# RWKV sample rows stored head by head and loaded with one transfer behind the first four cache pages

## The chip, the cores and the metric

The kernel runs on one core of a Trainium2 chip. A core has TensorE (PE: matrix products and transposes), VectorE (DVE), ScalarE (ACT) and GpSimd (POOL), and SyncE (SP), which here does nothing but wait on semaphores and issue DMA transfers; sixteen DMA engines move the data between the chip's main memory (DRAM or HBM) and the on-chip SBUF. The metric is the device time of one execution in microseconds (us). Two kernels are told apart by medians over several runs.

## The reference

One inference step of a two-layer hybrid trunk for a prompt of 256 tokens and for eight sample sequences of four tokens each. Each layer has three branches (SSD, RWKV-7, latent attention), gated and merged, and then a convolutional feed-forward network. Everything is float32. The part around the change is the RWKV recurrence of the sample sequences, and the paged attention of the same sequences that runs beside it:

```
D_MODEL, DEPTH, DEC_BATCH, DEC_SEQ = 1024, 2, 8, 4
RWKV_HEADS, RWKV_HEAD_DIM = 16, 64
PAST_LEN, PAGE_SIZE, MLA_KV_RANK, MLA_ROPE = 2048, 128, 256, 64     # 16 pages a sequence
def step(s, inp):                                  # rwkv_mixer, one token, state (b, h, v, k)
    r_t, w_t, k_t, v_t, kk_t, a_t = inp            # six vectors of 64 for each sequence and head
    sa = jnp.einsum('bhvk,bhk->bhv', s, -kk_t)
    s = (s * w_t[:, :, None, :] + sa[..., None] * (kk_t * a_t)[:, :, None, :]
         + v_t[..., None] * k_t[:, :, None, :])
    return s, jnp.einsum('bhvk,bhk->bhv', s, r_t)
s_fin, y = lax.scan(step, s0, (tm(rh), tm(wh), tm(kh), tm(vh), tm(kk), tm(ah)))
...                                                # then a normalization per head, bonus, gate
def page_step(carry, phys):                        # sample_mla: one page of 128 cached keys
    c, kr = lat_pool[phys], rope_pool[phys]
    k = mla_keys(c, kr, p['mla_w_kb'], p['mla_k_norm_g'])
    return update(carry, jnp.einsum('bqhe,blhe->bhql', q, k) * scale, c), None
carry, _ = lax.scan(page_step, init, page_table.T)
```

## The kernel before

`hybrid_trunk` loops over the two layers on the chip. A layer is a row of stages, each a block in which every engine has its own written list of instructions; engines wait for each other by named semaphores, and all of them meet at a barrier between two blocks. The order of work on an engine is therefore the order of the code. Four stages matter here, in this order.

`mla_prompt` is the attention of the prompt. Beside it TensorE transposes the sample tokens' six RWKV vectors, and VectorE copies them into `sample_rows` (32 rows, 6 vectors, 1024 columns). SyncE waits for the twelve copies (`row_kept`), stores the rows to the DRAM scratch `scratch_vec` (L707) and waits until they have landed; the block ends no earlier.

`mla_absorb` is short; SyncE loads the page table there.

`cache_attention` is the paged attention: eight sequences of 16 pages. Pages live in two slots, each a whole sequence, with four semaphores of four pages each. SyncE's `load(b, slot, g)` reads four page numbers and issues two transfers a page (L1052 latents, 128 KB; L1053 rotary keys, 32 KB). It loads both slots first, 32 pages, then the RWKV vectors into `vec` (L1060: 48 transfers, one for each sequence and vector, each of 16 heads by 4 tokens by 64), then `rwkv_state` (L1062, 2 MB), and then, as TensorE frees them, the pages of the other six sequences. For each page TensorE transposes (L1087, L1090), makes keys (L1112) and scores (L1116); ScalarE and VectorE square and sum the keys; the softmax of a sequence is done in pieces beside the pages of the next one (`finish`), and for the last sequence in a tail of its own, up to L1152. POOL waits for all 49 transfers (`rows_back`) and then runs the whole recurrence (`rwkv_sample_pool`, 304 instructions) on 128 partitions, one for each sequence and head, sequence-major. When it is done, SyncE stores the state (L1070).

`ssd_project` streams eleven weight blocks of 1 MB through a ring of three: SyncE loads, ScalarE rounds (L284), VectorE takes the rest (L290), TensorE multiplies (L297 to L299). Between them SyncE stores the normalized RWKV output `vec_y` to `scratch_y` in eight transfers (L1352), and loads it back as rows (L1356) for TensorE, which transposes it after the fifth block.

Of the kernel before, what the change touches and what calls it, by code (L numbers as in the profile page):

```python
# [28 lines left out]
P = 128  # L29
# [4 lines left out]
NB = 8  # L34
NS = 4
# [649 lines left out]
def mla_prompt(nc, k):  # L685
# [3 lines left out]
    with Stage(nc) as st:  # L689
# [13 lines left out]
        with st.block() as block:  # L703
            @block.sync
            def _(sp):
                sp.wait_ge(row_kept, 12)
                sp.dma_start(k.d["scratch_vec"].rearrange("t n d -> t n d"), rows[:, :, :]).then_inc(rows_out, 16)  # L707
                sp.wait_ge(rows_out, 16)

            @block.tensor  # L710
            def _(pe):
# [245 lines left out]
def cache_attention(nc, k):  # L957
# [19 lines left out]
    with Stage(nc) as st:  # L977
# [67 lines left out]
        with st.block() as block:  # L1045
            @block.sync
            def _(sp):
                def load(b, slot, g):
                    for j in range(4 * g, 4 * g + 4):
                        page = sp.value_load(k.pages[0:1, ds(b * PAGES + j, 1)], min_val=0, max_val=NPOOL - 1)  # L1050
                        row = ds(page, 1)
                        sp.dma_start(lat[:, slot, j, 0:KVRANK], k.ldram("cache_kv_latent")[row].rearrange("o p r -> (o p) r")).then_inc(in_l[slot][g], 16)  # L1052
                        sp.dma_start(kpe[:, slot, j, :], k.ldram("cache_k_rope")[row].rearrange("o p r -> (o p) r")).then_inc(in_l[slot][g], 16)  # L1053
                for slot in range(2):
                    for g in range(4):
                        load(slot, slot, g)

                for b in range(NB):
                    for n in range(6):
                        sp.dma_start(k.vec[16 * b:16 * b + 16, n, :, :],  # L1060
                                     k.d["scratch_vec"][NS * b:NS * b + NS, n, :].rearrange("t (h d) -> h t d", d=64)).then_inc(rows_back, 16)
                sp.dma_start(k.state[:, :, :], k.ldram("state_rwkv").rearrange("b h v k -> (b h) v k")).then_inc(rows_back, 16)  # L1062
                with sp.Fori(1, NB // 2) as i:
                    for slot in range(2):
                        for g in range(4):
                            sp.wait_ge(outed, i * (2 * GROUPS) + ((slot - 2) * GROUPS + g // 2 + 1))
                            load(i * 2 + slot, slot, g)

                sp.wait_ge(pool_step, POOL_STEPS)
                sp.dma_start(k.ldram("s_rwkv").rearrange("b h v k -> (b h) v k"), k.state[:, :, :]).then_inc(rwkv_out, 16)  # L1070
                sp.wait_ge(rwkv_out, 16)

            @block.gpsimd
            def _(pool):
                pool.wait_ge(rows_back, 16 * (6 * NB + 1))
                assert rwkv_sample_pool(nc, k, pool, pool_step) == POOL_STEPS

            @block.tensor
# [225 lines left out]
def ssd_project(nc, k):  # L1304
# [6 lines left out]
    with Stage(nc) as st:  # L1311
# [25 lines left out]
        with st.block() as block:  # L1337
            @block.sync
            def _(sp):
# [4 lines left out]
                for u in range(1, NU + 1):  # L1344
# [3 lines left out]
                                 w[:, ORDER[u] * G * P:(ORDER[u] + 1) * G * P].rearrange("(t p) n -> p t n", p=P)).then_inc(loaded[u % RING], 16)  # L1348
                    if u == RING - 1:
                        sp.wait_ge(normed, 1)  # L1350
                        for b in range(NB):
                            sp.dma_start(k.d["scratch_y"][NS * b:NS * b + NS, :].rearrange("t (h d) -> h t d", d=64),  # L1352
                                         k.vec_y[16 * b:16 * b + 16, :, :]).then_inc(y_out, 16)
                    if u == RING:
                        sp.wait_ge(y_out, 16 * NB)
                        sp.dma_start(sam_rows[:, :], k.d["scratch_y"]).then_inc(y_back, 16)  # L1356
                sp.wait_ge(rows_kept, 3)
                sp.dma_start(k.ldram("p_ssm_conv").rearrange("o j c -> (o j) c"), rows[0:3, :]).then_inc(stored, 16)
                sp.dma_start(k.ldram("s_ssm_conv").rearrange("b j c -> (b j) c"), rows[3:3 + 3 * NB, :]).then_inc(stored, 16)
# [1889 lines left out]

def hybrid_trunk(nc, dram):  # L3250
    k = Kit(nc, dram)
    with ExitStack() as ctx:
        def sb(name, shape, dt=F32):
            return ctx.enter_context(nc.sbuf_tensor(name, shape, dt))
# [57 lines left out]
```

## Time and profile before

| | |
|---|---|
| median of 3 runs | 3094.15 us (3092.66 to 3096.87) |
| span of the profiled execution | 3093.2 us |
| TensorE busy | 2765.1 us (89%) |
| VectorE, ScalarE, POOL busy | 1796.3, 1354.4, 840.5 us |
| cache attention, first layer | first page transfer at 460.53, last matmuls at 949.26 us |
| POOL's recurrence, first layer | 549.34 to 931.81 us |
| first transfer of the stage behind the prompt attention (`page_ids`) | 442.37 us |

The time of the profiled execution is its span, from the first to the last instruction, and what little lies around it; the span is 0.95 us under the median of the runs. Times in the rows are microseconds from the start of the span. PE is TensorE's matmuls, PEld its weight loads, a name with q behind it (SPq) the sequencer that issues DMAs. An instruction's row ends, in brackets, with the idle time before it and with whom it waited for.

### The profile page before, as it was taken

What the parts mean: (1) busy time and instruction counts of PE and PEld (TensorE: products, weight loads), DVE (VectorE), ACT (ScalarE), POOL (GpSimd) and SP (SyncE); (2) the same over time, 40 slices, a digit from 0 to 9 for tenths busy, and PEclk for the clock granted to TensorE, in tenths of its full rate; (3) what the DMA queues carried; (4) which work ended last, traced back from release to release, by engine and by line L of the source; (5) the groups of instructions that cost most, each with busy time, mean ns of one, the idle gap of its engine ahead of it and who ended that gap; (6) DMA issues with size and microseconds to landing.
All of it is one profiled execution on the core that took longest, in us unless ns stands there. A gap on an engine that the chain in (4) does not pass through costs nothing. (4 is left out here: it accounts for less than half of the span.)

```text
span 3093.2 us, 62907 instructions
## 1 busy us (share of the span) xinstructions
PE 2765.1 (89%) x24800; PEld 2537.1 (82%) x24800; DVE 1796.3 (58%) x3035; ACT 1354.4 (44%) x2174; POOL 840.5 (27%) x696
## 2 busy tenths in 40 slices
PE   7887779999997889899988867699999988898998
PEld 6876349999997779899977863499999886798998
DVE  4845454656655755499348453455565556554993
ACT  4733344445444343354356334344454443433542
POOL 0030000899990400000000300009999804000000
PEclk9999979999998989999989998799999989999999
DMA  5302102211115276465453021131211142764644
GB/s 132 101 5 81 46 15 75 63 50 54 35 35 177 71 197 166 106 163 139 119 123 84 4 80 46 26 92 39 57 43 39 54 157 78 204 164 109 163 134 119
DMA packets 471235, 281.94 MB, mean 91 GB/s; under 512 B 65294, under 2 KB 466489, under 8 KB 470315
## 3 DMA queue, kind: packets, MB, share of 16 engines
q1 hardware_dynamic: 468724, 276.85, 32.2%
q8 instruction: 190, 3.11, 0.4%
q10 hardware_dynamic: 2232, 1.26, 0.2%
q14 instruction: 89, 0.72, 0.1%
HBM read 258.75 MB, written 19.29 MB: 90 GB/s over the span
## 5 line engine op out<-in xcount | busy, mean ns | idle before, releaser
L1112 PE MATMUL key_banks<-w_kb_head,latent_T_head 128*128 128x352 f32 x1536 | 518.8, 338 | 0.0
L1112 PE MATMUL key_banks<-w_kb_rest,latent_T_head 128*128 128x352 f32 x1536 | 497.0, 324 | 0.0
L1112 PE MATMUL key_banks<-w_kb_head,latent_T_rest 128*128 128x352 f32 x1536 | 496.6, 323 | 0.0
L290 DVE TENSOR_TENSOR w_rests<-w_ring,w_heads 128x2048 fp32r<-128x2048 f32 (+1 forms) x152 | 326.3, 2149 | 163.9 <-ACT w_heads L284 163.7
L931 POOL TENSOR_TENSOR rwkv_state_tmp<-rwkv_state,vec 128x1024 f32<-128x1024 f32 x64 | 153.3, 2395 | 654.0 <-DMA rwkv_state<-in_state_rwkv_dram 649.1
L1257 DVE TENSOR_REDUCE w_kb<-key_sq 128x8 f32<-128x1024 f32 x256 | 309.3, 1208 | 0.0
L1172 ACT CAST latent_T_head<-turn_bank 128x256 fp32r<-128x256 f32 x256 | 95.5, 373 | 471.3 <-PE turn_bank L1090 298.5
L284 ACT CAST w_heads<-w_ring 128x2048 fp32r<-128x2048 f32 (+1 forms) x152 | 272.2, 1793 | 61.1 <-ACT conv_last_rows L1798 19.7
L1112 PEld LDWEIGHTS key_banks<-w_kb_rest,latent_T_head 128*128 128x128 f32 x1536 | 291.3, 190 | 0.0
L1112 PEld LDWEIGHTS key_banks<-w_kb_head,latent_T_head 128*128 128x128 f32 x1536 | 290.7, 189 | 0.0
L1112 PEld LDWEIGHTS key_banks<-w_kb_head,latent_T_rest 128*128 128x128 f32 x1536 | 290.0, 189 | 0.0
L2713 POOL TENSOR_TENSOR L_level<-L,const 128x1024 f32<-128x1024 f32 x24 | 56.3, 2367 | 855.8 <-DVE L L2719 802.5
L1188 ACT ACTIVATE key_sq<-key_banks 128x1056 f32<-128x1056 f32 x256 | 273.1, 1067 | 8.4 <-PE key_banks L1116 8.4
L1243 DVE TENSOR_TENSOR latent_T_rest<-turn_bank,latent_T_head 128x256 fp32r<-128x256 f32 x256 | 108.3, 423 | 269.4 <-ACT w_kb L1174 185.6
L297 PE MATMUL ffn_banks<-h_heads_T,w_heads 128*128 128x288 f32 x704 | 212.7, 302 | 17.1 <-DVE h_rests_T L1814 13.8
L298 PE MATMUL ffn_banks<-h_rests_T,w_heads 128*128 128x288 f32 x704 | 209.5, 298 | 0.0
L299 PE MATMUL ffn_banks<-h_heads_T,w_rests 128*128 128x288 f32 x704 | 208.6, 296 | 0.0
L934 POOL TENSOR_TENSOR rwkv_state_tmp<-rwkv_state_tmp 128x512 f32<-128x512 f32 (+4 forms) x320 | 196.7, 615 | 25.1
L297 PE MATMUL merge_banks<-out_heads,w_heads 128*128 128x288 f32 x512 | 152.1, 297 | 5.2 <-DVE out_rests L1620 5.2
L298 PE MATMUL merge_banks<-out_rests,w_heads 128*128 128x288 f32 x512 | 152.4, 298 | 0.0
L299 PE MATMUL merge_banks<-out_heads,w_rests 128*128 128x288 f32 x512 | 152.3, 297 | 0.0
L297 PEld LDWEIGHTS ffn_banks<-h_heads_T,w_heads 128*128 128x128 f32 x704 | 133.2, 189 | 21.5 <-DVE w_rests L290 17.8
(567 smaller groups left out, 7140.1 us busy)
## 6 DMA issues: line engine op xcount, KB each, us to landing
w_ring<-in_ffn_w_up_dram SPq DMA_DIRECT2D x88, 512.0 KB, 4.9
latents<-in_cache_kv_latent_dram SPq DMA_DIRECT2D x256, 128.0 KB, 2.0
w_ring<-in_w_in_dram SPq DMA_DIRECT2D x52, 512.0 KB, 3.7
w_ring<-in_w_gate_dram SPq DMA_DIRECT2D x48, 512.0 KB, 3.9
w_ring<-in_w_in_dram SPq DMA_DIRECT2D x20, 1024.0 KB, 6.0
w_ring<-in_ffn_w_down_dram SPq DMA_DIRECT2D x32, 384.0 KB, 3.6
w_ring<-in_ffn_w_down_dram SPq DMA_DIRECT2D x32, 320.0 KB, 4.1
rope_keys<-in_cache_k_rope_dram SPq DMA_DIRECT2D x256, 32.0 KB, 1.8
```

Of the source, the lines that this page charges most:

```text
L284: nc.scalar.copy(heads[:, slot, 0:tiles * P], ring[:, slot, 0:tiles * P]).then_inc(rounded, 1)
L290: ops.tensor_tensor(rests[:, slot, 0:tiles * P], ring[:, slot, 0:tiles * P], heads[:, slot, 0:tiles * P].bitcast(F32), ALU.subtract).then_ ...
L297: nc.tensor.matmul(out, wh, xh, start=start, stop=False)
L298: nc.tensor.matmul(out, wh, xl, start=False, stop=False)
L299: return nc.tensor.matmul(out, wl, xh, start=False, stop=stop)
L931: c(nc.gpsimd.tensor_tensor(tmp, S, over_v(n, t), ALU.mult))
L934: c(nc.gpsimd.tensor_tensor(tmp[:, :, 0:w], tmp[:, :, 0:w], tmp[:, :, w:2 * w], ALU.add))
L1112: last = nc.tensor.matmul(kbank[:, 3 * x + n, 0:KB], c[:, x, r * P:(r + 1) * P], w[:, r, cols], start=r == 0 and m == 0, stop=r == 1 and m ...
L1172: last = nc.scalar.copy(ch[:, x, :], xbank[:, 0:2 * P])
L1188: nc.scalar.activation(sq[:, x, :], kbank[:, 3 * x:3 * x + 3, 0:KB], ACT.Square).then_inc(squared, 1)
L1243: nc.vector.tensor_tensor(cl[:, x, :], xbank[:, 0:2 * P], ch[:, x, :].bitcast(F32), ALU.subtract).then_inc(t_kept, 1)
L1257: nc.vector.tensor_reduce(ss[:, slot, j, :], sq[:, x, f:f + KW].rearrange("p (h e) -> p h e", e=NOPE), AX.X, ALU.add).then_inc(summed, 1)
```

## The change

The scratch tensors get another layout and the partitions of `vec`, `rwkv_state` and `vec_y` another order. In `scratch_vec` a vector is now kept head by head (vector, head, row, 64 columns) and in `scratch_y` the output likewise (head, row, 64). SBUF partitions count head-major (head, then sequence), not sequence-major. With that, `vec` is loaded by one transfer with 1 KB pieces, in place of 48. The rows are stored by six transfers in place of one, in pieces of 64 values; the state is loaded and stored by eight transfers, one for each sequence; `vec_y` is stored by one in place of eight and loaded back in 64-value pieces. And the loads of `vec` and `rwkv_state` move forward: they stand behind the first four pages of slot 0, ahead of the other 28.

```
@@ mla_prompt, block.sync
                 sp.wait_ge(row_kept, 12)
-                sp.dma_start(k.d["scratch_vec"].rearrange("t n d -> t n d"), rows[:, :, :]).then_inc(rows_out, 16)
-                sp.wait_ge(rows_out, 16)
+                for n in range(6):
+                    sp.dma_start(k.vec_rows[n].rearrange("h r d -> r h d"),
+                                 rows[:, n, :].rearrange("r (h d) -> r h d", d=64)).then_inc(rows_out, 16)
+                sp.wait_ge(rows_out, 96)
@@ cache_attention, block.sync
+                load(0, 0, 0)
+                sp.dma_start(k.vec[:, :, :, :].rearrange("p n t d -> p n (t d)"),
+                             k.vec_rows.rearrange("n h (b t) d -> (h b) n (t d)", b=NB)).then_inc(rows_back, 16)
+                for b in range(NB):
+                    sp.dma_start(k.state[b:P:NB, :, :].rearrange("p v k -> p (v k)"),
+                                 k.ldram("state_rwkv")[b:b + 1].rearrange("b h v k -> (b h) (v k)")).then_inc(rows_back, 16)
                 for slot in range(2):
-                    for g in range(4):
+                    for g in range(1 - slot, 4):
                         load(slot, slot, g)
-
-                for b in range(NB):
-                    for n in range(6):
-                        sp.dma_start(k.vec[16 * b:16 * b + 16, n, :, :],
-                                     k.d["scratch_vec"][NS * b:NS * b + NS, n, :].rearrange("t (h d) -> h t d", d=64)).then_inc(rows_back, 16)
-                sp.dma_start(k.state[:, :, :], k.ldram("state_rwkv").rearrange("b h v k -> (b h) v k")).then_inc(rows_back, 16)
...
                 sp.wait_ge(pool_step, POOL_STEPS)
-                sp.dma_start(k.ldram("s_rwkv").rearrange("b h v k -> (b h) v k"), k.state[:, :, :]).then_inc(rwkv_out, 16)
-                sp.wait_ge(rwkv_out, 16)
+                for b in range(NB):
+                    sp.dma_start(k.ldram("s_rwkv")[b:b + 1].rearrange("b h v k -> (b h) (v k)"),
+                                 k.state[b:P:NB, :, :].rearrange("p v k -> p (v k)")).then_inc(rwkv_out, 16)
+                sp.wait_ge(rwkv_out, 16 * NB)
@@ cache_attention, block.gpsimd
-                pool.wait_ge(rows_back, 16 * (6 * NB + 1))
+                pool.wait_ge(rows_back, 16 * (1 + NB))
@@ ssd_project, block.sync
                         sp.wait_ge(normed, 1)
-                        for b in range(NB):
-                            sp.dma_start(k.d["scratch_y"][NS * b:NS * b + NS, :].rearrange("t (h d) -> h t d", d=64),
-                                         k.vec_y[16 * b:16 * b + 16, :, :]).then_inc(y_out, 16)
+                        sp.dma_start(k.y_by_head.rearrange("h (b t) d -> (h b) t d", b=NB), k.vec_y[:, :, :]).then_inc(y_out, 16)
                     if u == RING:
-                        sp.wait_ge(y_out, 16 * NB)
-                        sp.dma_start(sam_rows[:, :], k.d["scratch_y"]).then_inc(y_back, 16)
+                        sp.wait_ge(y_out, 16)
+                        sp.dma_start(sam_rows[:, :].rearrange("r (h d) -> r h d", d=64), k.y_by_head.rearrange("h r d -> r h d")).then_inc(y_back, 16)
@@ hybrid_trunk
+    k.vec_rows = dram["scratch_vec"].rearrange("r n c -> (r n c)").rearrange("(n h r d) -> n h r d", n=6, h=16, d=64)
+    k.y_by_head = dram["scratch_y"].rearrange("r c -> (r c)").rearrange("(h r d) -> h r d", h=16, d=64)
```

SyncE's order is all that moves; the other engines' lists keep theirs. At the start of the cache attention, before the change, SyncE goes from the last of the 32 pages (latents and rotary keys) to the 48 vector loads and the state, and then into the loop over the later sequences:

```order
L1052 DMA latents<-in_cache_kv_latent_dram 128x256
L1053 ISA
L1053 DMA rope_keys<-in_cache_k_rope_dram 128x64
L1060 DMA vec<-scratch_vec 16x4x64 x48
L1062 ISA
L1062 DMA rwkv_state<-in_state_rwkv_dram 128x4096
L1063 UNCONDITIONAL_BRANCH
```

After the change, these are the rows behind the fourth page; the transfer pair of `rwkv_state` stands eight times, of which two are shown here, and page 4 follows (TENSOR_LOAD reads its number):

```order
L1054 DMA latents<-in_cache_kv_latent_dram 128x256
L1055 ISA
L1055 DMA rope_keys<-in_cache_k_rope_dram 128x64
L1057 DMA vec<-scratch_vec 128x6x256
L1060 ISA
L1060 DMA rwkv_state<-in_state_rwkv_dram 16x4096
...
L1060 ISA
L1060 DMA rwkv_state<-in_state_rwkv_dram 16x4096
L1052 TENSOR_LOAD page_ids
```

What moved: 49 transfers behind 32 pages became nine transfers behind four pages, ahead of 28.

In the SSD projection, before the change, the eight stores stand between the third and the fourth weight block (`w_ring`):

```order
L1347 DMA w_ring<-in_w_in_dram 128x8x256
L1352 DMA scratch_y<-vec_y 16x4x64 x8
L1347 ISA
L1347 DMA w_ring<-in_w_in_dram 128x8x256
L1356 DMA sam_y_rows<-scratch_y 32x1024
```

After it, one store stands there:

```order
L1351 DMA w_ring<-in_w_in_dram 128x8x256
L1355 DMA scratch_y<-vec_y 128x256
L1351 ISA
L1351 DMA w_ring<-in_w_in_dram 128x8x256
L1358 DMA sam_y_rows<-scratch_y 32x16x64
```

The places are the same; seven transfers ahead of the fourth block are gone, and the load back has smaller pieces.

## Rows read from the trace of the kernel before

**Rows 1.** Waits, whole execution (us in total, times, longest).
```profile
POOL rwkv_state_tmp L931 <- DMA rwkv_state<-in_state_rwkv_dram: 649.1, 2, 325.3
```

**Rows 2.** SyncE timeline, cache attention (start us, us, instruction).
```profile
460.53 0.37 SPq L1052 DMA_DIRECT2D latents<-in_cache_kv_latent_dram  x1
...
466.37 0.33 SPq L1053 DMA_DIRECT2D rope_keys<-in_cache_k_rope_dram  x1
...
467.53 0.33 SPq L1052 DMA_DIRECT2D latents<-in_cache_kv_latent_dram  x1
...
517.23 23.91 SPq L1060 DMA_DIRECT2D vec<-scratch_vec  x48
```

**Rows 3.** POOL timeline, first and last of the layer.
```profile
549.34 2.38 POOL L931 TENSOR_TENSOR rwkv_state_tmp<-rwkv_state,vec 128x1024 f32<-128x1024 f32 x1 [323.78 <-DMA rwkv_state<-in_state_rwkv_dram]
...
931.59 0.22 POOL L936 TENSOR_TENSOR vec_y<-rwkv_state_tmp 128x16 f32<-128x16 f32 x1
```

**Rows 4.** TensorE timeline, page 4's transposes and the stage's last matmuls.
```profile
483.02 0.42 PE L1087 MATMUL turn_bank<-const,latents 128*128 128x128 f32 x2
...
949.26 5.78 PE L1152 MATMUL misc_bank<-qa,w_vb 128*128 128x32 f32 x32 [0.71 <-DVE qa L1294]
```

**Rows 5.** DMA issues (line, count, KB each, median us to landing).
```profile
rope_keys<-in_cache_k_rope_dram SPq DMA_DIRECT2D x256, 32.0 KB, 1.8
...
rwkv_state<-in_state_rwkv_dram SPq DMA_DIRECT2D x2, 2048.0 KB, 7.9
...
scratch_vec<-sample_rows SPq DMA_DIRECT2D x2, 768.0 KB, 5.3
...
out_dram<-kpe_tm SPq DMA_DIRECT2D x2, 64.0 KB, 1.7
...
out_dram<-kpe_tm SPq DMA_DIRECT2D x2, 8.0 KB, 1.4
```

**Rows 6.** Waits of TensorE, 457 to 956 us.
```profile
PE turn_bank L1087 <- DMA rope_keys<-in_cache_k_rope_dram: 12.2, 1, 12.2
...
PE misc_bank L1124 <- DVE w_kb L1280: 7.1, 1, 7.1
...
PE misc_bank L1127 <- ACT w_kb L1213: 3.9, 8, 0.7
```

**Rows 7.** VectorE, lines L1271, L1276, 470 to 956 us (ns min/median/max).
```profile
L1271 DVE TENSOR_TENSOR w_kb<-w_kb,rope_sumsq x8: 279/754/2482, 533.0 to 935.2; 128x128 f32<-128x128 f32 x8
...
L1276 DVE TENSOR_TENSOR w_kb<-w_kb x8: 681/1270/2535, 542.8 to 937.6; 128x512 f32<-128x512 f32 x8
```

**Rows 8.** Windows (stretch, busy us of each engine, clock, DMA share, GB/s).
```profile
517.00:541.00 24.00, 24.00 (x164) 24.00 (x163) 13.35 (x24) 14.57 (x26) 0.00 (x0) 1.00 0.18 39
541.30:549.30 8.00, 8.00 (x55) 8.00 (x55) 6.07 (x10) 3.07 (x6) 0.00 (x0) 1.00 0.75 268
693.00:711.00 18.00, 17.91 (x124) 17.80 (x124) 10.80 (x20) 9.31 (x17) 17.06 (x13) 1.00 0.35 92
```

**Rows 9.** Second layer: SyncE's first page transfer, TensorE's transposes of page 4.
```profile
1998.50 0.38 SPq L1052 DMA_DIRECT2D latents<-in_cache_kv_latent_dram  x1
...
2020.12 0.41 PE L1087 MATMUL turn_bank<-const,latents 128*128 128x128 f32 x2
```

**Rows 10.** Prompt attention: SyncE's rows store, ScalarE's last copy.
```profile
433.09 0.34 SPq L707 DMA_DIRECT2D scratch_vec<-sample_rows  x1
...
441.35 0.37 ACT L777 COPY o_mla<-attn_banks 128x256 f32<-128x256 f32 x1 [0.46 <-PE attn_banks L745]
```

**Rows 11.** SSD projection: SyncE, ScalarE, VectorE around the fourth weight block.
```profile
966.45 3.62 SPq L1352 DMA_DIRECT2D scratch_y<-vec_y  x8
...
975.55 1.91 ACT L284 CAST w_heads<-w_ring 128x2048 fp32r<-128x2048 f32 x1 [4.13 <-DMA w_ring<-in_w_in_dram]
...
977.57 2.29 DVE L290 TENSOR_TENSOR w_rests<-w_ring,w_heads 128x2048 fp32r<-128x2048 f32 x1 [0.23 <-ACT w_heads L284]
```

**Rows 12.** Waits of TensorE, 956 to 1035 us.
```profile
PE ssd_banks L297 <- DVE w_rests L290: 1.3, 1, 1.3
```

## The prediction

> **What bounds the kernel now.** I read the list of waits of the whole execution first, since the change is about what one engine waits for. GpSimd (POOL) waits 649.1 us in two waits for the DMA that loads `rwkv_state` [rows 1]: the largest wait that the change touches. The question is whether anybody waits for POOL in turn.
>
> So next the SyncE queue at the start of the cache-attention stage. The reader sees the first page's transfer at 460.53, page 3's last at 466.37, page 4's first at 467.53, and the 48 small `vec` transfers only at 517.23, taking 23.91 us to issue [rows 2]. POOL therefore starts at 549.34 and ends at 931.59 + 0.22 = 931.8 [rows 3]. TensorE's last work in the same stage starts at 949.26 and takes 5.78 us [rows 4], so the stage ends at about 955, and POOL's end lies 23 us before it. The state's store, issued right after POOL, still has to fit in those 23 us; the load of the same 2 MB takes 7.9 us to land [rows 5], so it does, with some 15 us to spare. The list counts two such waits, one in each layer.
>
> The waits of TensorE in that stage say the same: 12.2 us at its start for the first four pages, 7.1 us in the tail for VectorE, 3.9 us in eight pieces for ScalarE [rows 6]. None is POOL, and none is a DMA after the first page. The stage is TensorE's own matmuls. One thing POOL does cost others: two VectorE operations with both inputs in SBUF take 279 and 681 ns at best and 2482 and 2535 ns at worst [rows 7]. But TensorE has no wait of that size in the middle of the stage [rows 6], so this is absorbed now.
>
> **The change part by part.**
>
> *POOL starts earlier.* The vec load (one transfer) and the state load (eight) are issued behind page 3, at 466.7. A vec transfer is issued in 23.91 / 48 = 0.50 us [rows 2]; nine issues at that price are 4.5 us. The data: 0.79 MB of vec in 1 KB pieces. In a stretch of page loads the engines were busy 0.35 of 18 us at 92 GB/s, which is 263 GB/s while they move, so 3.0 us; the state load kept them busy 0.75 of 8.0 us, 6.0 us [rows 8]. Beginning some 1.3 us after the first issue, 9.0 us of data end at about 477, and POOL starts near 478 instead of 549.3: 71 us earlier, and ends near 861. Worth on the path: 0, since 23 us lie between POOL's end and the stage's end today and the path does not pass through it. By the same argument the state's store (now eight transfers, behind the last page load) moves under the matmuls: 0. Below zero it can't be, as nothing in the tail waits for either.
>
> *Page 4 comes later.* This is the price of the new place, and what is queued behind it on SyncE is all later pages. Four pages are issued in 467.53 - 460.53 = 7.0 us. Page 7's last issue was at 460.53 + 7.0 + 5.84 (the offset of 466.37) = 473.4; with 4.5 us more it is 477.9, and with 0.3 us of issue and 1.8 us to landing [rows 5] the second group is complete at 480.0. The nine transfers' data are through at 477 and do not bind. TensorE asks for page 4 at 483.02, 22.5 us after the first issue; in the second layer at 2020.12, 21.6 us after 1998.50 [rows 4, 9]. So 3.0 and 2.1 us are left: 0. Over the stage TensorE takes (949.3 - 460.5) / 128 = 3.8 us a page and SyncE 1.75, so behind this group the gap only grows. Upper end: if the data moved at half the speed, 18 us from 468 on would end at 486, and the group's 0.66 MB would take another 5 us: 8 to 9 us late in each layer. I take 0, as both speeds come from rows of the same transfers.
>
> *The rows are stored head by head.* Where one transfer of 32 rows of 24 KB stood, six are issued, in pieces of 256 B: 3072 pieces, 192 for each of 16 DMA engines. The prompt's attention ends with SyncE's wait for them, and every engine waits for SyncE at the barrier behind it. Now the store is issued at 433.09 and lands 5.3 us later, at 438.4; ScalarE ends the stage at 441.35 + 0.37 = 441.7 [rows 5, 10]. Cover: 3.3 us. The new price: the 3072 pieces of today's vec loads kept the engines busy 0.18 of 24 us, that is 0.18 x 24 x 16 / 3072 = 22.5 ns a piece [rows 8]. Those are reads; for writes the two stores of `kpe_tm` have 16 and 2 such pieces for each engine and take 1.7 and 1.4 us [rows 5], so 0.3 / 14 = 21 ns. The sum is 1.4 + 192 x 0.0225 = 5.7 us; by issue, five times 0.5 us before the last, then 1.4 + 0.7, it is 4.6. The larger counts: landing at 438.8, still 2.9 us under ScalarE. Cost 0. Lower end 0 as well, since the present wait isn't on the path. Upper end: twice the price per piece, 10.0 us, lands at 443.1 and costs 1.4 us a layer. I take 0 because the writes' own rows agree with the reads'.
>
> The Trainium skill ("DMA: Bandwidth & Descriptors", Specifications) speaks against this edit: it says that below 512 B a transfer is done as a read and a write back, off the line rate. The trace doesn't decide it, because 14 pieces in 0.3 us is a coarse reading. By that rule the price per piece would at least double, which is the upper end above.
>
> *The sample output (`vec_y`).* Eight stores become one and the load back is now in 256 B pieces. The eight hold SyncE for 3.62 us from 966.45, and the weight load behind them is the one ScalarE waits 4.13 us for, until 975.55. About 3.2 us of it goes. What is late next: VectorE splits that weight block at 977.57, after only 0.23 us of idle time, since it was busy with the convolution until then [rows 11]. So 3.2 us on ScalarE shrink to 0.2 on VectorE; and TensorE waits in this stage once for a weight split in the running part, 1.3 us, for an earlier block [rows 12]. Worth 0; the other end is 3.2 us a layer if TensorE were hungry there. The load back has several units of time before it is asked for: 0.
>
> *Sum.* 0 on a profiled span of 3093.2 us. Before and after that span lies under 1 us, as the median of three runs is 3094.15. I forecast the median: 3094.
>
> **The rivals.**
> *Slower, by the rows' store.* One mechanism: 256 B writes to HBM so dear that SyncE holds the barrier at the end of the prompt attention. It begins to cost at (441.7 - 433.1 - 1.4) / 192 = 38 ns a piece. At three times the price, 67 ns, the store takes 14.4 us and lands at 447.5: 5.8 us a layer, 11.6 in all, 3106. To pass what counts as slower it takes 54 ns. For it: no row has so many small writes at once. Against: the 21 ns. Chance 0.08.
> *Slower, by a starved first turn.* The half-speed case above: 17 us, 3111. Against it stand two rows of the very transfers. It would need a backlog of over 13 us in place of 9. Chance 0.03.
> *Faster, by the output rows.* The 3.2 us of both layers reach TensorE: 3088. For it: ScalarE did wait 4.13 us. Against: VectorE's 0.23. Chance 0.04.
> *Faster, by POOL.* If POOL set the stage's end, up to its 23 us tail could be used better. The trace has no one waiting for it: 0.01, 3080 at best.
> *The change doesn't move POOL.* If the state load lands late, POOL may start at 490 or 550: the time is the same, as the trace has 23 us of cover. It belongs to the main case.
>
> **How the numbers follow.** The main case has 0.84: 3094, with its small losses of up to 1.4 us at the barrier and 1 to 2 us at page 4 in each layer reaching 3100, and its small gains 3091. About 0.2% (6 us) is what a measurement of this kernel can tell from no change. Faster: 0.04 + 0.01 = 0.05. Slower: of 0.11 in the two slow cases about 0.01 stays below the bound, 0.10. Same: 0.85. The range 3089 to 3101 leaves out the far parts of both.
>
> **What would show it.** In the changed profile POOL's first `rwkv_state` operation stands at about 478 and its last at about 861; TensorE's waits in the stage are the same three, with no wait of its page transposes for a DMA after the first page; the stage still takes some 495 us. The six `scratch_vec` stores are issued from 433.1 in some 2.7 us and the next stage's `page_ids` load stays within 0.5 us of 442.4. ScalarE's 4.13 us before 975.55 shrink to about 1. I am wrong if `page_ids` moves by 2 us or more, if TensorE waits for `rope_keys` twice in a layer, or if the stage gets shorter by more than 3 us.

## The result and the profile after

| | before | changed |
|---|---|---|
| median of the runs | 3092.24 us (17 runs, 3086.7 to 3098.3) | 3100.70 us (17 runs, 3094.8 to 3105.6) |
| ratio, with its 95% interval | | 1.0025 [1.0018, 1.0033] |
| span of the profiled execution | 3093.2 us | 3099.6 us |
| POOL's recurrence, first layer | 549.34 to 931.81 us | 489.53 to 872.30 us |
| TensorE's wait for page 4, first and second layer | none, none | 2.0, 0.8 us |

The changed kernel is slower by 0.25%, some 8 us, where no change was forecast. In a second comparison it was 1.0014 [1.0005, 1.0023] (experiment 5). POOL is earlier by 60 us and waits for the state in two waits that sum to 517.1 us in place of 649.1 [rows 1]; that bought nothing, as forecast. What the profile shows as new is TensorE's wait for page 4.

The two profiled executions differ by 6.4 us, but 5.5 us of that stand before the first changed instruction: the rows' store is issued at 438.63 where it was at 433.09 [rows 10]. From the first page transfer of the cache attention to the first weight transfer of the SSD projection, the two layers' stages took 496.97 and 497.07 us after (965.16 - 468.19 in the first), 496.06 and 495.12 before: 2.9 us more, which is the two waits.

SyncE's timeline after (start us, us, instruction), which answers to [rows 2]:

```profile
468.19 0.38 SPq L1054 DMA_DIRECT2D latents<-in_cache_kv_latent_dram  x1
...
474.43 0.43 SPq L1057 DMA_DIRECT2D vec<-scratch_vec  x1
475.05 5.37 SPq L1060 DMA_DIRECT2D rwkv_state<-in_state_rwkv_dram  x8
481.27 0.35 SPq L1054 DMA_DIRECT2D latents<-in_cache_kv_latent_dram  x1
481.86 0.33 SPq L1055 DMA_DIRECT2D rope_keys<-in_cache_k_rope_dram  x1
483.41 0.34 SPq L1054 DMA_DIRECT2D latents<-in_cache_kv_latent_dram  x1
484.00 0.34 SPq L1055 DMA_DIRECT2D rope_keys<-in_cache_k_rope_dram  x1
485.17 0.33 SPq L1054 DMA_DIRECT2D latents<-in_cache_kv_latent_dram  x1
...
487.45 0.33 SPq L1055 DMA_DIRECT2D rope_keys<-in_cache_k_rope_dram  x1
```

Page 4 is issued 13.1 us after the first page (481.27 - 468.19), where it was 7.0. Eight state transfers take 5.37 us to issue, 0.67 from one to the next; and behind page 4 SyncE loses another 0.4 us (481.86 to 483.41 is 1.55 us, the same step a page later, 484.00 to 485.17, is 1.17). The last transfer of pages 4 to 7, for which TensorE waits as one group, is issued at 487.45.

TensorE's timeline after, transposes of pages 2, 3, 4 and 5 (in brackets the idle time before), which answers to [rows 4]:

```profile
482.94 0.41 PE L1091 MATMUL turn_bank<-const,latents 128*128 128x128 f32 x2
486.31 0.41 PE L1091 MATMUL turn_bank<-const,latents 128*128 128x128 f32 x2
491.79 0.41 PE L1091 MATMUL turn_bank<-const,latents 128*128 128x128 f32 x2 [2.03 <-issue]
495.19 0.42 PE L1091 MATMUL turn_bank<-const,latents 128*128 128x128 f32 x2
```

TensorE asks for page 4 at 489.76, 21.6 us behind the first issue, and gets it at 23.6. "issue" stands where the profile names no releaser; that it is the page's DMA is what experiments 1, 2 and 4 show. In the second layer the same wait is 0.8 us:

```profile
PE turn_bank L1091 <- DMA rope_keys<-in_cache_k_rope_dram: 12.2, 1, 12.2
...
PE turn_bank L1091 <- issue: 0.8, 1, 0.8
```

The window from the `vec` load's issue to POOL's start, after (columns as in [rows 8]):

```profile
474.40:489.50 15.10, 12.16 (x70) 11.80 (x70) 4.33 (x8) 3.73 (x8) 0.00 (x0) 0.77 0.98 229
```

The DMA engines are busy 0.98 of these 15 us and move only 229 GB/s. In [rows 8] they moved 268 GB/s at a share of 0.75, 357 while busy. This is where the forecast went wrong: it had taken the state's data at the speed of [rows 8].

The other two edits, after: the six row stores and the next stage's first transfer on SyncE, then ScalarE's last copy of the stage, which answer to [rows 10]:

```profile
438.63 3.36 SPq L708 DMA_DIRECT2D scratch_vec<-sample_rows  x6
449.23 0.26 SPq L842 DMA_DIRECT2D page_ids<-in_page_table_dram  x1
```

```profile
448.21 0.37 ACT L779 COPY o_mla<-attn_banks 128x256 f32<-128x256 f32 x1 [0.30 <-PE attn_banks L747]
```

`page_ids` stands 0.65 us behind the end of ScalarE's copy, and before it was 442.37 - 441.72 = 0.65 too: the barrier still waits for ScalarE. The rows' store, ScalarE's copy and `page_ids` are all later than before, by 5.5, 6.9 and 6.9 us, so the shift of `page_ids` isn't made by the store. In the SSD projection ScalarE's wait for the fourth weight block:

```profile
981.78 1.91 ACT L284 CAST w_heads<-w_ring 128x2048 fp32r<-128x2048 f32 x1 [1.66 <-DMA w_ring<-in_w_in_dram]
```

It is 1.66 us where it was 4.13 [rows 11].

### The profile page after: what moved, and what is told of

The parts are those of the page before. It is cut to its first block and busy times, and to the rows that moved or that the text cites. A ratio compares the mean times of both kernels' runs of the same rounds, so it can differ in the third digit from the quotient of the medians.

```text
span 3099.6 us, 62879 instructions
## 1 busy us (share of the span) xinstructions
PE 2768.2 (89%) x24800; PEld 2538.6 (82%) x24800; DVE 1801.8 (58%) x3035; ACT 1354.6 (44%) x2174; POOL 839.5 (27%) x696
## 5 line engine op out<-in xcount | busy, mean ns | idle before, releaser
L933 POOL TENSOR_TENSOR rwkv_state_tmp<-rwkv_state,vec 128x1024 f32<-128x1024 f32 x64 | 153.8, 2404 | 521.9 <-DMA rwkv_state<-in_state_rwkv_dram 517.1
```

The lines of the kernel that those rows point to most:

```text
L933: c(nc.gpsimd.tensor_tensor(tmp, S, over_v(n, t), ALU.mult))
```

## Experiments

A piece is one packet of a transfer as the trace records it; a partition of the state is one piece of 16 KB. Its mean duration was 725 ns (most at 611) in the load before and 618 in the store before; in the changed kernel it was 1196 and 1143, so the state's load takes 128 x 1.196 / 16 = 9.6 us of the sixteen engines in place of 5.8. Ratios are to the kernel before, run on the same chip. In the edits, lines that only follow from those shown (the counts in the semaphore waits, the load back in experiment 3) are left out.

**1. The loads behind all 32 pages** (new layout and transfers, old place).

```
-                load(0, 0, 0)
+                for slot in range(2):
+                    for g in range(4):
+                        load(slot, slot, g)
...
```

> The changed kernel with the loads of vec (one transfer) and of the state (eight) put back behind all 32 pages; all else as changed. Theory A, the new place is what costs (pages 4 to 7 come late): the time is that of the kernel before, ratio 1.000 within 0.001. Theory B, the smaller pieces or the eight state transfers cost wherever they stand (at the barrier behind the prompt attention or in the SSD projection): the ratio stays at 1.0025. In the profile POOL starts about 20 us earlier than before (SyncE saves some 20 us of issue), no wait of TensorE's page transposes behind the first page.

Measured: 1.0000 [0.9987, 1.0012], 3095.04 us. TensorE has no page-4 wait in either layer, though the state's pieces still take 1.20 us. So the new layout, the row stores, the single `vec` load and the output path cost nothing that can be measured, nor gain (the interval leaves room for some 4 us either way): the loss appears only with the new place.

**2. The loads behind eight pages.**

```
                 load(0, 0, 0)
+                load(0, 0, 1)
...
-                    for g in range(1 - slot, 4):
+                    for g in range(2 - 2 * slot, 4):
```

> The changed kernel with the loads of vec and state behind the first eight pages of slot 0, not four. Theory A (pages 4 to 7 come late, nothing else): ratio 1.000; TensorE asks for page 8 some 13 us after page 4, and the backlog of about 13 us of data starts 7 us later, so no wait. Theory C, POOL beside the first pages costs by itself (POOL still starts some 60 us earlier than before): ratio 1.0025 as in the changed kernel. Theory B (layout): also 1.0025.

Measured: 1.0006 [0.9993, 1.0019], 3094.74 us; no wait for pages in either layer, and POOL's two waits are 529.3 us, 12 more than in the changed kernel. Four pages later the same data and the same issues are hidden.

**3. The output path as before** (eight stores of `vec_y`, one load back), the rest as changed.

```
-                        sp.dma_start(k.y_by_head..., k.vec_y[:, :, :]).then_inc(y_out, 16)
+                        for b in range(NB):
+                            sp.dma_start(k.d["scratch_y"][NS * b:NS * b + NS, :]..., k.vec_y[b:P:NB, :, :]).then_inc(y_out, 16)
```

> The changed kernel with the path of the sample output in the SSD projection as it was: eight stores of vec_y in row layout and one load back of whole rows. Theories A and C: ratio stays near 1.0025, since the y path is worth nothing in either direction. Theory B in its form that the y path costs: ratio back to 1.000.

Measured: 1.0011 [0.9999, 1.0022], 3097.43 us, with a page-4 wait of 0.8 us in both layers. The interval holds both no change and the changed kernel's second ratio, so by time it is inconclusive. TensorE's timeline shows why this execution lost little:

```profile
483.20 0.41 PE L1091 MATMUL turn_bank<-const,latents 128*128 128x128 f32 x2
487.43 0.41 PE L1091 MATMUL turn_bank<-const,latents 128*128 128x128 f32 x2 [0.80 <-issue]
```

The first page was issued at 463.90 here, so page 4 came at 23.5 us as in the changed kernel (23.6), but TensorE asked at 22.7, not 21.6. The arrival is nearly fixed (23.5 to 23.6 in these two executions); the asking moves by 1 us with how soon the clock rises over the first pages: the granted clock went from 0.50 to 1.00 13.1 us behind the first issue in the changed kernel's first layer, and 15.9 us behind it here.

**4. The state in one transfer of 128 partitions.** Its partitions are then in the old order, so the recurrence runs on the states of other sequences and heads; work and sizes are the same.

```
-                for b in range(NB):
-                    sp.dma_start(k.state[b:P:NB, :, :]..., k.ldram("state_rwkv")[b:b + 1]...).then_inc(rows_back, 16)
+                sp.dma_start(k.state[:, :, :], k.ldram("state_rwkv").rearrange("b h v k -> (b h) v k")).then_inc(rows_back, 16)
```

> The changed kernel with the state loaded by one transfer over all 128 partitions in place of eight over 16 partitions each; same bytes, same place. The load ignores the new partition order, so the sample recurrence computes with states of other sequences and heads. In the profile of the changed kernel a 16 KB piece of the state took 1196 ns on its DMA engine, against 725 in the kernel before. Theory A1, the state's data are dear because a transfer over every eighth partition reaches too few write ports of SBUF: pieces back at 600 to 750 ns, the backlog falls from 13 to about 9 us, POOL starts some 9 us after the issue as forecast, TensorE waits less than 0.5 us for page 4, ratio 1.000. Theory A2, pieces are slow because pages, vec and state share the engines there, whatever the partitions: pieces stay near 1200 ns and the wait for page 4 stays at 1 to 2 us, ratio 1.002 or more.

Measured: 1.0003 [0.9991, 1.0014], 3093.98 us; no page-4 wait in either layer; the pieces are at 611 ns. The window of the state's data:

```profile
473.60:479.10 5.50, 5.34 (x26) 5.37 (x27) 0.42 (x1) 0.37 (x1) 0.00 (x0) 0.65 1.01 419
```

The same 2 MB go by at 419 GB/s. Place and `vec` are as in the changed kernel, so what starves page 4 is the state's eight transfers: their extra data (9.6 us against 128 x 0.615 / 16 = 4.9 here, by the mean piece) or their extra issue (seven more at 0.67, 4.7 us).

**5. The changed kernel again.**

> The changed kernel itself, beside the others of this set. The waits that the profile showed for page 4 sum to 2.0 + 0.8 us less the overlap, 3.0 us in both layers. If they are the whole loss, the ratio to the kernel before is 1.0010 (some 3096 to 3097 us), and 1.0025 of the first comparison was partly luck of the executions. If something else of 3 us or more is lost in executions that no profile caught, the ratio is again 1.002 to 1.003 (3100 to 3102).

Measured: 1.0014 [1.0005, 1.0023], 3099.14 against 3095.35 us. Between the two expectations; the profile of this run says why they were both too simple:

```profile
490.39 0.66 PE L1091 MATMUL turn_bank<-const,latents 128*128 128x128 f32 x2 [2.20 <-issue]
495.33 0.41 PE L1091 MATMUL turn_bank<-const,latents 128*128 128x128 f32 x2
...
2029.50 0.42 PE L1091 MATMUL turn_bank<-const,latents 128*128 128x128 f32 x2 [1.83 <-issue]
2034.43 0.41 PE L1091 MATMUL turn_bank<-const,latents 128*128 128x128 f32 x2
```

From page 4 to page 5 it is 4.94 us here, in both layers; 3.40 in the first profile of the same kernel. The granted clock of the two executions behind the wait, first the changed kernel's first profile, then this one:

```profile
491.00:493.00 2.00, 1.21 (x9) 1.24 (x10) 0.08 (x1) 0.65 (x3) 1.92 (x2) 1.00 0.30 88
493.00:495.00 2.00, 2.00 (x14) 2.00 (x13) 1.46 (x3) 0.85 (x1) 1.76 (x4) 1.00 0.47 106
```

```profile
491.00:493.00 2.00, 2.00 (x9) 2.00 (x8) 0.60 (x3) 1.50 (x3) 1.84 (x3) 0.50 0.28 82
493.00:495.00 2.00, 2.00 (x12) 2.00 (x11) 1.14 (x2) 0.00 (x0) 1.69 (x5) 0.81 0.33 88
```

Behind a wait of some 2 us TensorE's clock can be down from 2.4 to 1.2 GHz (1.00 to 0.50 in the seventh column), and then the wait costs 1.5 us more than itself. In the profiles that have no wait for page 4 (before, and experiments 1, 2, 4, 8, 10 and 11, two layers each) the granted clock stays at 1.00 there. This execution lost 2.20 + 1.83 + 2 x 1.54 = 7.1 us at page 4, the first profile 2.0 + 0.8 = 2.8. The two stages together took 997.4 us here (498.84 and 498.52, measured as above), 994.0 in the first profile, and 990.0 to 993.2 in the seven without the wait.

**6. The nine loads from ScalarE's queue.**

```
@@ block.sync
-                sp.dma_start(k.vec..., k.vec_rows...).then_inc(rows_back, 16)
-                for b in range(NB):
-                    sp.dma_start(k.state[b:P:NB, :, :]..., k.ldram("state_rwkv")[b:b + 1]...).then_inc(rows_back, 16)
@@ block.scalar, ahead of its first page
+                act.dma_start(k.vec..., k.vec_rows...).then_inc(rows_back, 16)
+                for b in range(NB):
+                    act.dma_start(k.state[b:P:NB, :, :]..., k.ldram("state_rwkv")[b:b + 1]...).then_inc(rows_back, 16)
```

> The changed kernel with the nine loads (vec, and the state in eight) issued from ScalarE's queue beside the first pages' squares, so that SyncE's page transfers have nothing queued behind them on their own queue; the data still meet the pages' data on the DMA engines. If page 4's lateness is a matter of the order in SyncE's queue, its wait is gone in both layers and the ratio is 1.0000. If it is a matter of DMA bandwidth, whatever the queue, the 9.6 us of state data still stand in the way of pages 5 to 12: TensorE waits 1 us or more for a page in a layer, and the ratio stays near 1.001. The price is 9 issues on ScalarE, 5 us, which has idle time there.

Measured: 1.0072 [1.0057, 1.0088], 3118.60 us: outside both. ScalarE reached the loads at 463.2, ahead of SyncE's first page (464.18), so their data ran beside the first four pages, on which TensorE waits anyway. ScalarE's queue, and TensorE's first page:

```profile
463.20 0.40 ACTq L1163 DMA_DIRECT2D vec<-scratch_vec  x1
463.78 1.32 ACTq L1166 DMA_DIRECT2D rwkv_state<-in_state_rwkv_dram  x2
```

```profile
482.10 0.69 PE L1086 MATMUL turn_bank<-const,latents 128*128 128x128 f32 x2 [22.53 <-DMA rope_keys<-in_cache_k_rope_dram]
```

That wait is 22.5 and 21.4 us in the two layers, 12.2 before [rows 6]: 19.5 us of the 23 lost. The page-4 wait is gone. Ahead of the first pages, where TensorE is waiting already, the data cost it 10.3 and 9.2 us; in experiment 2, four pages behind the changed kernel's place, nobody pays for the same data.

**7. The kernel before with its own 49 loads behind the first four pages**: the change of place without the new layout.

```
+                load(0, 0, 0)
...
-                    for g in range(4):
+                    for g in range(1 - slot, 4):
```

> The kernel before, with its own 48 vec loads and its one state load moved behind the first four pages: the change of place alone, without the new layout. Theory (the order on SyncE starves TensorE at page 4): 49 issues are 24.4 us; page 4's group was complete at 15.0 us behind the first page's issue, is now complete at 39.4 or a little later behind the state's 5.9 us of data, and is asked for at 22.5 and 21.6: TensorE waits 17 us in the first and 18 us in the second layer, nothing is caught up later, and the time is 3093 + 35 = 3128, ratio 1.011. Rival (TensorE's wait is caught up later in the stage, from the pages already loaded): under 1.005.

Measured: 1.0140 [1.0119, 1.0160], 3136.67 us: 41 us, where 35 were expected.

```profile
498.35 0.66 PE L1087 MATMUL turn_bank<-const,latents 128*128 128x128 f32 x2 [17.45 <-issue]
504.10 0.41 PE L1087 MATMUL turn_bank<-const,latents 128*128 128x128 f32 x2
...
2056.20 0.66 PE L1087 MATMUL turn_bank<-const,latents 128*128 128x128 f32 x2 [16.56 <-issue]
2061.35 0.42 PE L1087 MATMUL turn_bank<-const,latents 128*128 128x128 f32 x2
```

The waits are 34.0 us, where 35 were expected, and the pages behind them take 5.75 and 5.15 us in place of 3.4: the clock again, 4.1 us. Nothing is caught up later; the last 3 of the 41 us stay open and lie within the interval (37 to 50 us). Beside experiment 4, which has the same state load at the same place but one `vec` load for 48 and is at 1.0003, it shows what affords the move at all: the single `vec` load.

**8. The state into neighbours, the store from every eighth partition** (kernel before, old place, eight transfers each).

```
-                sp.dma_start(k.state[:, :, :], k.ldram("state_rwkv")...)
+                for b in range(NB):
+                    sp.dma_start(k.state[16 * b:16 * b + 16, :, :], k.ldram("state_rwkv")[b:b + 1]...)
...
+                for s in range(8):
+                    sp.dma_start(k.ldram("s_rwkv")...[s:P:8], k.state[s:P:8, :, :])
```

> The kernel before, but the state goes in eight transfers of 16 partitions each, at the old place: the load into 16 neighbouring partitions from 16 neighbouring rows of HBM, the store from every eighth partition to every eighth row. The changed kernel's pieces of 16 KB took 1.20 us (load) and 1.14 us (store), the kernel before's 0.72 and 0.62 us. Theory of the SBUF side (how far a transfer's partitions are spread sets its rate): 16 neighbouring partitions are the narrowest choice, so the load's piece takes longer than 1.2 us, some 2.4 us if half as many ways in halve the rate again, and the store's stays near 1.14. Rival on the HBM side (16 neighbouring rows at once are slow): load 1.2 us, store from and to rows 128 KB apart back at 0.6. Rival that eight transfers are slow as such, whatever they reach: 1.2 for both.

Measured (one profiled execution): load 1.95 us a piece, 104 of 128 pieces at 2.0 to 2.1; store 1.14, as in the changed kernel although its HBM rows now lie 128 KB apart. The load's window:

```profile
541.00:557.00 16.00, 15.54 (x107) 15.39 (x106) 10.08 (x18) 6.19 (x12) 0.00 (x0) 1.00 0.92 116
```

116 GB/s. The load has the same HBM rows as in the changed kernel and other partitions, and is slower. The store has the same partitions and other HBM rows, and is the same. The SBUF side decides.

**9. The state by one transfer into the right partitions**, early.

```
-                for b in range(NB):
-                    sp.dma_start(k.state[b:P:NB, :, :]..., k.ldram("state_rwkv")[b:b + 1]...)
+                sp.dma_start(k.state[:, :, :]..., k.ldram("state_rwkv").rearrange("b h v k -> h b (v k)"))
```

> The changed kernel with the state loaded by one transfer into the right partitions (head first, then sequence), at the new place; all else as changed. Theory (the loss is page 4's wait, which comes from eight transfers into 16 partitions each, and from the clock that falls in some executions behind such a wait): the state's pieces are back from 1.2 to 0.6 or 0.7 us, seven issues of 0.67 us are gone, TensorE doesn't wait for page 4 in either layer, POOL still starts behind page 4, and the ratio is 1.0000 to 1.0003. Rival (part of the loss is in the rows' store or in POOL running beside the first pages, which this keeps): the ratio stays at 1.001 or more. It can't be under 0.9995 by either, since nobody waits for POOL.

Measured: 1.0018 [1.0002, 1.0034], 3101.02 us. The theory that the number of partitions in a transfer sets the rate fell: all 128 are in one transfer, and its pieces still take 1.21 us, 95 of 128 at 1.2 to 1.3. The window of its data, and TensorE's page 4 and 5 in the first and second layer:

```profile
476.90:487.40 10.50, 10.50 (x59) 10.50 (x59) 2.82 (x7) 3.21 (x6) 0.00 (x0) 0.80 1.01 217
```

```profile
490.55 0.41 PE L1090 MATMUL turn_bank<-const,latents 128*128 128x128 f32 x2 [1.74 <-issue]
493.92 0.42 PE L1090 MATMUL turn_bank<-const,latents 128*128 128x128 f32 x2
...
2027.77 0.66 PE L1090 MATMUL turn_bank<-const,latents 128*128 128x128 f32 x2 [2.62 <-issue]
2032.53 0.42 PE L1090 MATMUL turn_bank<-const,latents 128*128 128x128 f32 x2
```

It also parts what experiment 4 left together. Seven issues are gone here (page 4 is issued 8.4 us behind the first page, not 13.1), the slow data are not, and page 4 is as late as ever: at 23.85 us. So the slow data are enough for the whole lateness, and the seven issues add nothing to it. In both kernels the group of pages 4 to 7 is complete 3.2 to 3.4 us behind the end of the state's last piece (487.35 here, 488.44 in the changed kernel, by the pieces in the trace): its data stand behind the state's. The extra issues with fast data were not run; by an estimate from the rows, the group's last issue at 19.3 us behind the first, with 0.3 of issue and 1.8 to landing, would be there at 21.4, just ahead of TensorE's asking.

**10. Every eighth partition for the load, neighbours for the store** (as 8, swapped).

```
+                for s in range(8):
+                    sp.dma_start(k.state[s:P:8, :, :], k.ldram("state_rwkv")...[s:P:8])
...
+                for b in range(NB):
+                    sp.dma_start(k.ldram("s_rwkv")[b:b + 1]..., k.state[16 * b:16 * b + 16, :, :])
```

> The kernel before, the state in eight transfers at the old place, the other way round than in the last look: the load into every eighth partition from every eighth row of HBM, the store from 16 neighbouring partitions to 16 neighbouring rows. There the load into neighbours took 1.95 us for a piece of 16 KB and the store from every eighth partition 1.14 us. If the partitions decide, the load is now at 1.2 us and the store at 1.8 to 2.0. If loads into neighbouring partitions are slow for a reason of the load alone, the store stays near 1.14. If the HBM rows decided, the load from rows 128 KB apart would be at 0.6 to 0.7.

Measured: load 1.17 us, from rows 128 KB apart, which ends the HBM rival. The store's mean is 1.27, not the 1.8 to 2.0 expected: 24 pieces at 0.6, some 16 at 2.1 to 2.5, the rest between. Here the store from neighbours suffers less than the load into them; why stays open.

**11. Partitions seven apart** (as 8, load and store alike; the last 16 are neighbours).

```
+                for s in range(7):
+                    sp.dma_start(k.state[s:112:7, :, :], k.ldram("state_rwkv")...[s:112:7])
+                sp.dma_start(k.state[112:P, :, :], k.ldram("state_rwkv")...[112:P])
```

> The kernel before, at the old place, the state in seven transfers of 16 partitions each that lie seven apart (s, s+7, ..., s+105) and an eighth into the last 16, load and store alike. Pieces of 16 KB took 1.2 us with 16 partitions eight apart, 1.95 (load) with 16 neighbours, and 1.21 in one transfer of all 128 whose 16 heads were shared out over the DMA engines, partitions 8h + b in step. Theory (what counts is on how many of SBUF's ways in the 16 partitions lie that are written at the same moment; by the port rule of the SBUF page, which I work out here for 16 partitions eight apart, they reach 8 ports, neighbours 4, seven apart 14): the pieces of the seven transfers are near 0.6 to 0.9 us, most at 0.61, and only the last 16 near 1.2 to 2.1. Rival (a transfer of 16 partitions is slow whatever they are, and the one of 128 was slow for its HBM side): 1.2 again.

Measured: load 0.95 us in the mean, 92 of 128 pieces under 1.0; store 82 of 128 at 0.61, mean 0.89 with the last 16. Transfers of 16 partitions need not run at 1.2 us: it depends on which 16. The load is at the upper end of what was expected, and not at 0.61.

What follows from 8 to 11: about sixteen pieces of the state are under way at the same time, and their rate depends on which partitions they belong to. By what most pieces take, full rate (0.61 us) is 128 partitions in their own order; half rate (1.25) is every eighth, in eight transfers or in experiment 9's one; under a third (2.07 in experiment 8) is 16 neighbours. The Trainium skill ("SBUF — State Buffer", Door 1: The DMA port swizzle) states a map that fits, 16 ports chosen by bits of the partition number. By an estimate from it, every eighth partition reaches 8 ports and 16 neighbours 4, which would make factors of 2 and 4; the pieces show 2.05 and 3.4. Seven apart reaches 14 or 15, one or two partitions to a port; the measured factors are 1.6 in the load and near 1 in most of the store. The Trainium skill ("DMA: Bandwidth & Descriptors", The descriptor swizzle) says that in a plain transfer of 128 partitions each engine writes one port; the 0.61 us of that form agree. The Trainium skill (the same page, Why a DMA increments its semaphore by 16 and not by 1) says that the number of engines is the largest up to 16 that divides the outermost dimensions of both sides. Experiment 9's source has the 16 heads outermost. If each engine takes one head, then partitions 8h + b are written in step, the same spread as every eighth, and 1.21 us agrees. This reading is argued, not shown: no trace tells a piece's partition or port.

## Why the prediction was wrong

*POOL starts earlier, worth 0.* Right in kind. The start was at 21.3 us behind the first page, not 17.5, for the reason below; the end at 872.3 lies 85 us before TensorE's last work of the stage at 957.81. The state's store is issued only at 894.5, behind the last pages, and is hidden all the same.

*Page 4 comes later, cost 0.* This is the step that failed, and in it one term: "the state load kept them busy 0.75 of 8.0 us, 6.0 us [rows 8]". That row is one transfer of 128 partitions in their order, and the change replaces it by eight of 16 partitions eight apart; the prediction took "both speeds" to "come from rows of the same transfers". The pieces take 1.20 us in place of 0.72: 9.6 us of the engines, not 6.0. A second term was short too: nine issues took 6.1 us (13.1 - 7.0), not 4.5. The group was forecast complete 19.5 us behind the first issue and came at 23.6; TensorE asks at 21.6 to 22.7, so the slack of 3.0 and 2.1 us became waits of 2.0 and 0.8. Experiment 9 shows that the data term alone makes the whole lateness, and 4 that with fast data and fewer issues the wait is gone. The upper end for half the speed stood in the text (8 to 9 us late, 17 us in all): the speed came out near it, but the price was overdrawn, since the 9 us of `vec` and state data were doubled to 18, and only the state's were slow. `vec`'s 768 pieces of 1 KB at some 58 ns make 2.8 us, so it was 12.4 us; and the pages' group behind it, put at 5 us, took 3.2 to 3.4. The last missing piece is that a wait of 2.2 us cost 3.7, because the clock fell behind it.

How large the loss is: two profiled executions of the changed kernel hold 2.8 and 7.1 us at page 4, and the two comparisons 5.6 to 10.2 and 1.5 to 7.1 us. The two comparisons overlap at 5.6 to 7.1. What the profiles account for is thus 3 to 7 us an execution, and whether the first comparison's 8 us hold more than that is left open: the first profiled execution took 3101.42 us, above its kernel's median, with only 2.8 us at page 4, and the seven profiled spans of kernels without a page-4 wait (before, and experiments 1, 2, 4, 8, 10, 11) spread from 3090.8 to 3097.1 us for reasons that no run here separates. Experiments 1 and 2 leave no room for another loss of 6 us or more.

The measured 3100.7 us lie inside the stated 3089 to 3101, and that is in part luck. The range's top was made of 1.4 us at the barrier and 1 to 2 us at page 4 in each layer; the barrier cost nothing, and page 4 cost about what was allowed there, or twice that where the clock fell. The forecast itself, no change, was wrong.

*The signs.* Two of those named for being wrong appeared. TensorE waited a second time for pages in each layer, which was the loss. `page_ids` moved by 6.9 us, far over the 2 named, but with ScalarE's copy and not by the rows' store; that sign was badly chosen, since an absolute time carries everything that the execution lost before it. The distance to ScalarE's end, 0.65 us in both, was the one to watch.

*The rows stored head by head, cost 0.* Right. The 3072 pieces of 256 B took 18.7 ns each (22.5 was the estimate), the last began at 443.7, and ScalarE ended at 448.58. The Trainium skill ("DMA: Bandwidth & Descriptors", Specifications) puts transfers below 512 B off the line rate, as a read and a write back. The first half agrees: 256 B in 18.7 ns is 13.7 bytes a ns, where the state's 16 KB in 0.615 us is 26.6. A doubled price over the estimate, which the prediction drew from it, did not come; such stores cost about what such loads do (17 ns a piece in the 48 `vec` loads before).

*The output rows, gain 0.* Right. ScalarE's wait shrank by 2.5 us, of 3.2 forecast, and nothing of it reached the time: TensorE's wait for the split of a weight block in that stage is 1.6 us, where it was 1.3 [rows 12], and experiment 1, which has this edit, is at 1.0000.

*The rivals.* The case that occurred is the starved first turn, at a third to a half of its price. It was said to need a backlog of over 13 us; one of 12.4 was enough for a small loss. It was held unlikely by "two rows of the very transfers", and that was the error.

## What to carry to other kernels

When one transfer is replaced by several over strided or fewer partitions, its old rate is no estimate: look at which partitions the engines write at the same moment, and measure a piece. Loads that nobody is waiting for belong behind the transfers that have slack to lose, and the slack is to be counted in data on the DMA engines, not only in the order of a queue: here four more pages ahead cost POOL, which had 23 us to spare, some 6 us a layer, and left no loss that could be measured. And a new wait of TensorE of some 2 us can cost nearly twice its length: here the clock was down behind three of the five waits between 1.7 and 2.7 us.

## What the runs showed of the hardware

- A state transfer's 16 KB piece, by what most take: 0.61 us (128 partitions in order), 1.25 (16 partitions eight apart), 2.07 (16 neighbours, load; the mean of all is 1.95); seven apart it is 0.95 in the load's mean. While busy, the sixteen engines moved 419 GB/s in the first (experiment 4), 217 at the second's pieces (experiment 9) and 126 (116 / 0.92) in the third (experiment 8).
- HBM rows 16 KB or 128 KB apart make no difference to this: means of 1.20 and 1.17 us in the load, 1.14 and 1.14 in the store (changed kernel, experiments 8 and 10).
- TensorE's granted clock behind a wait for page 4: it fell to 0.50 after waits of 1.8 and 2.2 us (experiment 5), 2.6 (experiment 9) and 17 (experiment 7), and not after 0.8, 1.7 (experiments 3 and 9) and 2.0 (changed kernel); where it fell, the next page took 4.8 to 5.8 us in place of 3.4.
- From one issue to the next on SyncE it was 0.67 us for a 16-partition state load (5.37 / 8, changed kernel) and 0.50 for one of the 48 `vec` loads (23.91 / 48, before).
